# Head norms of the queries as row scales of the softmax, and two reordered activations in the cells of a two-block fp32 layer stack

## The reference

```python
q = rms_norm(q.reshape(b_, t_, ATT_HEADS, ATT_HD), qn_g)      # 8 query heads of 64
k = rms_norm(k.reshape(b_, t_, ATT_KV_HEADS, ATT_HD), kn_g)   # 2 key heads of 64
if tabs is not None:
    q, k = rope_2d(q, tabs), rope_2d(k, tabs)
...
s = jnp.einsum('bqkgd,bskd->bkgqs', q, k).astype(jnp.float32) * (ATT_HD ** -0.5)
p = jax.nn.softmax(s, axis=-1).astype(v.dtype)
```

## Time and profile before

| | |
|---|---|
| median of 3 runs | 3383.92 us (3381.69 to 3394.71) |
| the profiled execution | 3379.07 us, its span 3377.3 us |
| PE busy | 3191.2 us, 94% of the span |
| DVE, ACT, POOL busy | 1307.8, 834.7, 1599.3 us |
| chain that ended last | PE 83%, DVE 9%, POOL 3%, ACT 3%, issue 2% |
| ACT_TABLE_LOAD | 152, of 1283 ns each |

### The profile page before, as it was taken

One profiled execution on the slowest core, in us unless ns is written; L12 is line 12 of the kernel. 1 busy time (PEld: TensorE's weight loads), 2 busy tenths in 40 slices (PEclk: granted clock), 3 DMA queues, 4 the chain that ended last, 5 costly groups with the idle time before them and its releaser, 6 DMA issues.

```text
span 3377.3 us, 40269 instructions
## 1 busy us (share of the span) xinstructions
PE 3191.2 (94%) x15099; PEld 2291.8 (68%) x15099; DVE 1307.8 (39%) x2442; ACT 834.7 (25%) x1479; POOL 1599.3 (47%) x1507
## 2 busy tenths in 40 slices
PE   7999987999999999998989999999999999999988
PEld 4666655656666555465778768888984588889944
DVE  3021325545554412315666543444332334443321
ACT  4123235421111022325411112232110122321110
POOL 1788996000000059961354247775640287765600
PEclk9999989999999999999999999999999999999999
DMA  7111100024444121110234322222221222222211
GB/s 227 40 38 32 38 26 14 14 66 134 125 129 133 40 63 38 44 38 1 72 119 144 96 75 75 63 75 63 76 75 50 64 75 63 76 63 75 74 48 41
DMA packets 259332, 236.59 MB, mean 70 GB/s; under 512 B 20887, under 2 KB 257347, under 8 KB 259141
## 3 DMA queue, kind: packets, MB, share of 16 engines
q1 hardware_dynamic: 259140, 234.02, 22.8%
HBM read 231.91 MB, written 2.10 MB: 69 GB/s over the span
## 4 chain that ended last, share of the span: by engine, by line
PE 83%; DVE 9%; POOL 3%; ACT 3%; issue 2%; DMA 0%; DVEq 0%; ACTq 0%; SPq 0%; POOLq 0%
PE ps L466 29%; PE ps L1140 22%; PE ps L496 10%; PE ps L982 4%; DVE arena L1753 3%; PE ps L1184 2%; ACT arena L1277 2%; PE ps L745 2%; PE ps L1228 1%; PE ps L482 1%; DVE small L1962 1%; DVE bQz L1757 1%; PE ps L1086 1%; POOL arena L2364 1%; PE ps L1220 1%
## 5 line engine op out<-in xcount | busy, mean ns | idle before, releaser
L2364 POOL TENSOR_TENSOR arena<-arena,posi 128x512 f32<-128x512 f32 (+1 forms) x360 | 409.4, 1137 | 30.0
L466 PE MATMUL ps<-hT,wring 128*128 128x512 f32 (+1 forms) x1184 | 411.8, 508 | 1.2 <-ACT arena L1277 1.2
L496 PE MATMUL ps<-hT,wring 128*128 128x512 f32 (+1 forms) x1024 | 373.2, 519 | 1.2 <-ACT arena L1277 1.2
L466 PE MATMUL ps<-arena,wring 128*128 128x512 f32 (+1 forms) x992 | 367.9, 531 | 0.0
L466 PEld LDWEIGHTS ps<-hT,wring 128*128 128x128 f32 x1184 | 230.1, 196 | 169.7 <-issue 153.9
L1277 ACT ACTIVATE arena<-ps 128x256 f32<-128x256 f32 (+4 forms) x403 | 176.4, 438 | 656.2 <-PE ps L466 234.2
L2446 POOL TENSOR_TENSOR arena<-wring 128x512 f32<-128x512 f32 x72 | 92.7, 1288 | 475.5 <-PE ps L1140 292.7
L466 PEld LDWEIGHTS ps<-arena,wring 128*128 128x128 f32 x992 | 187.6, 190 | 175.2 <-issue 168.4
L496 PEld LDWEIGHTS ps<-hT,wring 128*128 128x128 f32 x1024 | 192.5, 192 | 152.3 <-issue 143.5
L1277 ACT ACT_TABLE_LOAD x152 | 195.0, 1283 | 371.8 <-DVE small L2250 85.8
L2363 POOL TENSOR_SCALAR posi<-arena,cols 128x512 f32<-128x512 f32 (+1 forms) x360 | 246.2, 684 | 35.4
(11 more groups left out here) (256 smaller groups left out, 4909.8 us busy)
## 6 DMA issues: line engine op xcount, KB each, us to landing
wring<-in_w_in SPq DMA_DIRECT2D x126, 1024.0 KB, 5.3
wring<-in_w_mod SPq DMA_DIRECT2D x24, 1024.0 KB, 8.3
wring<-in_w_out SPq DMA_DIRECT2D x24, 1024.0 KB, 5.7
wring<-in_w_ada SPq DMA_DIRECT2D x21, 1024.0 KB, 5.2
wring<-in_w_conv_out SPq DMA_DIRECT2D x7, 512.0 KB, 6.1
wring<-in_w_gla_out SPq DMA_DIRECT2D x7, 512.0 KB, 6.2
wring<-in_w_attn_out SPq DMA_DIRECT2D x7, 512.0 KB, 5.5
arena<-in_w_ada SPq DMA_DIRECT2D x3, 1024.0 KB, 5.1
```

Source lines behind the costliest of these rows:

```text
L466: last = eng.matmul(o_(out), a, b_, start=(i == 0), stop=(i == len(parts) - 1))
L496: mm = eng.matmul(bank[b][:, 0:n], w[:, k, j * P:(j + 1) * P], hT[:, k, t0:t0 + n], start=(k == 0), stop=(k == KD - 1))
L2364: pool.link(eng.tensor_tensor(dst, dst, scratch, ALU.add))
```

## The change

Query norms. The queries are no longer multiplied by their inverse root. Their tiles are turned raw, with the gain folded into the permutation (`gperm`), and the gain also goes into the product with the cosine. The inverse roots of all four query tiles (`qscale`, 128 tokens on the partitions by 6 blocks by 8 heads) come from one root and one reciprocal, and are used twice in the attention: the negated row maximum is multiplied by them (`nmax`, a product of 128 x 1 on DVE after each maximum), and ACT's exponential takes them as its scale. The keys stay normed, with one root and one reciprocal for both tiles. The GLA spread moves behind the second query turn, and DVE's products that use it (`gla_scaled`) with it. For the whole stretch the V ring has four banks (`HEAD_RINGS`).

Cells. For mLSTM heads `silu(n, 3)` stands between the two parts of the activation of the gate z instead of behind them. In every chunk ACT takes a root of `eps` into an unused column after it has emptied the chunk's product and before it waits for the variance.

```diff
-        hcol = sb("hcol", [P, 2, 6, 2])
+        kcol = sb("kcol", [P, 2, 6, 2])
+        head_cols = sb("head_cols", [P, NCH * 16])
+        qscale = head_cols[:, 0:48].rearrange("p (a b c) -> p a b c", b=6, c=2)
+        gperm = pt[:, 3, TX:TX + P]
+        k_squares, q_squares = [pt[:, 2, :], last_tile], [pr[:, 0, :], pr[:, 1, :], pt[:, 2, :], last_tile]
...
-        qcol = sb("qcol", [P, NCH, 4, 4])
+        qcol = head_cols.rearrange("p (a b c) -> p a b c", b=4, c=4)
...
-                gla_out_norm(l, 1, between)
+                next(between, None)
+                gla_square_sums(l, 1)
+                rings[0] = HEAD_RINGS
+
+                def head_sums(name, b, tiles_):
+
+                    pe.stage("attn_proj")
+                    key = (name + "ss", l)
+                    claim(b)
+                    eng.wait_ge(*at(("gla out read", l, 1)))
+                    for j in tiles_:
+                        eng.wait_ge(*at(("hsq", l, name, j)))
+                        for u in units(0 if name == "k" else l):
+                            src = (k_squares if name == "k" else q_squares)[j]
+                            last = eng.matmul(bank[b][:, 12 * j + 2 * u:12 * j + 2 * u + 2], src[:, u * P:(u + 1) * P],
+                                              const[:, K_HALF:K_HALF + P:64], start=True, stop=True)
+                    last.then_inc(*pe.tell(("full", key)))
+                    bank_of[key], last_on[b] = bank[b], key
+
...
+                            for i, u in enumerate(UNITS[sg]):
+                                for hf in range(2):
+                                    last = eng.matmul(o_[64 * hf:64 * hf + 64, i * P:(i + 1) * P],
+                                                      kcol[:, j, u, hf:hf + 1].broadcast_to([P, 64]), ident,
+                                                      start=True, stop=True)
+                            return last
+                        eng.wait_ge(*at(("k inverse", l)))
+                        job("V", ("hbc", l, j, sg), mms)
...
+                    pe.stage("attn_proj")
+                    if name == "k":
+                        src, perm = ak[:, j, TC:T], const[:, K_PERM:K_PERM + P]
+                        eng.wait_ge(*at(("normed", l, j)))
+                    else:
+                        src, perm = res[:, 8 + j, TC:T], gperm
+                        eng.wait_ge(*at(("q perm", l)))
+                        eng.wait_ge(*at(("free", ("aq", l, j, segs(l)[-1]))))
+                    job("V", ("rot", l, name, j), lambda o_: eng.matmul(o_[:, 0:TX], perm, src, start=True, stop=True))
+
+                head_sums("k", 4, (0, 1))
+                next(between, None)
+                key_norms(0)
+                key_norms(1)
+                turned("q", 0)
+                next(between, None)
+                turned("k", 0)
+                turned("k", 1)
+                head_sums("q", 7, range(4))
+                turned("q", 1)
+                next(between, None)
+                gla_spread(l, 1)
+                turned("q", 2)
+                next(between, None)
+                turned("q", 3)
                 pe.stage("attn_proj")
-
-                for t in range(len(HEAD_TILES) + 2):
-                    if t < len(HEAD_TILES):
-                        name, j = HEAD_TILES[t]
-
-                        def mms(o_):
-                            for u in units(0 if name == "k" else l):
-                                last = eng.matmul(o_[:, 2 * u:2 * u + 2], sq[t % 2][:, u * P:(u + 1) * P],
-                                                  const[:, K_HALF:K_HALF + P:64], start=True, stop=True)
-                            return last
-                        eng.wait_ge(*at(("hsq", l, name, j)))
-                        job("A", ("hss", l, name, j), mms)
-                    if t % 2:
-                        next(between, None)
-                        pe.stage("attn_proj")
...
@@ -1393,10 +1428,16 @@
                         fn(gsq[hh][:, t0:t0 + n].rearrange("p (a b) -> p a b", b=GLA_CHUNK), src, ACT.Square)
                     m.mark(("gla sq", l, 2 * p + hh), act.name, act.n[act.name])
                 m.mark(("gla out read", l, p), act.name, act.n[act.name])
+                if p:
+                    for j in range(2):
+                        fn(k_squares[j], ak[:, j, :], ACT.Square, ("hsq", l, "k", j))
                 next(between, None)
                 act.stage("gla_norm")
                 for hh in range(2):
                     evac(("gss", l, 2 * p + hh), gcol[:, hh, u0:6], u0, 6 - u0, ACT.Sqrt, scale=1.0 / P, bias=eps[:, :])
+                if p:
+                    act.stage("attn_proj")
+                    evac(("kss", l), kcol.rearrange("p a b c -> p (a b) c"), 0, 24, ACT.Sqrt, bias=eps[:, :])
...
+                eng.wait_ge(*at(("q inverse", l)))
+
                 def probabilities(n, e):
                     i = first + n
+                    sg, hp, qb = pairs[n]
+                    r = qscale[:, hp, UNITS[sg][qb], e:e + 1]
...
-                    fn(dst, src, ACT.Exp, ("probs", i, e), bias=small[:, 40 + z:41 + z], accum_out=small[:, 44 + z:45 + z])
+                    fn(dst, src, ACT.Exp, ("probs", i, e), scale=r, bias=small[:, 40 + z:41 + z], accum_out=small[:, 44 + z:45 + z])
...
-                for t in range(len(HEAD_TILES) + 2):
...
-                        if t > 1:
-                            eng.wait_ge(*at(("full", ("hss", l, *HEAD_TILES[t - 2]))))
-                        fn(sq[t % 2][:, u0 * P:T], src[:, u0 * P:T], ACT.Square, ("hsq", l, name, j))
-                        if t > 1:
-                            for sg in both if HEAD_TILES[t - 2][0] == "k" else segs(l):
-                                eng.wait_ge(*at(("full", ("hbc", l, *HEAD_TILES[t - 2], sg))))
-                        evac(("hss", l, name, j), hcol[:, t % 2, u0:6, :], 2 * u0, 12 - 2 * u0, ACT.Sqrt, bias=eps[:, :])
-                    next(between, None)
+                u0 = units(l)[0]
+                act.stage("attn_proj")
+                for j in range(4):
+                    src, dst = res[:, 8 + j, u0 * P:T], q_squares[j][:, u0 * P:T]
+                    fn(dst, src, ACT.Square, ("hsq", l, "q", j))
+                next(between, None)
+                act.stage("attn_proj")
+                eng.wait_ge(*at(("full", ("qss", l))))
+                src = bank_of["qss", l][:, 0:48].rearrange("p (a b) -> p a b", b=12)[:, :, 2 * u0:12]
+                fn(qscale.rearrange("p a b c -> p a (b c)")[:, :, 2 * u0:12], src, ACT.Sqrt, ("free", ("qss", l)), bias=eps[:, :])
...
                             evac(key, zt_flat[:, 0:HALF], 0, HALF, ACT.Silu)
+                            if not r:
+                                silu(n, 3)
                             eng.wait_ge(*at(("free", ("right", (l, n, i)))))
                             fn(zt_flat[:, HALF:], zt_flat[:, HALF:], ACT.Silu, ("gate z", l, n))
-                        if not r and i:
+                        if not r and 0 < i < 4:
                             silu(n, i - 1)
...
                         evac(("intra", k), NI[:, 0:W], 0, W)
+                        fn(small[:, 90:91], eps[:, :], ACT.Sqrt)
                         eng.wait_ge(*at(("var", k)))
                         fn(small[:, 56:57], small[:, 55:56], ACT.Sqrt, ("sd", k), bias=eps[:, :])
...
-                            dve.link(eng.tensor_reduce(small[:, 40 + z:41 + z], src, ax, ALU.max, negate=True), ("nmax", i, e))
+                            nmax = small[:, 40 + z:41 + z]
+                            sg, hp, qb = pairs[n]
+                            dve.link(eng.tensor_reduce(nmax, src, ax, ALU.max, negate=True))
+                            tt(nmax, nmax, qscale[:, hp, UNITS[sg][qb], e:e + 1], M_, ("nmax", i, e))
...
-                    out_norm(l, p)
-                m.mark(("branch", l, 1), *m.at[("gla out done", l, 1)])
+                    if p == 0:
+                        out_norm(l, p)
...
+                gain = small[:, 20 + l:21 + l]
+                ts(gain, col(l, QN), 0.125, None, M_, None)
+                eng.wait_ge(*at(("gla core", (l, 1, 1))))
+                ts(gperm, const[:, K_PERM:K_PERM + P], gain, None, M_, None, ("q perm", l))
+                gla_inverse(l, 1)
+                dve.stage("rope")
+                eng.wait_ge(*at(("free", ("kss", l))))
+                rcp(kcol[:, :, :, :], kcol[:, :, :, :], ("k inverse", l))
+                for j in range(2):
+                    for sg in ("x", "c"):
+                        s0, n = SEG[sg]
+                        k = ("hbc", l, j, sg)
+                        eng.wait_ge(*at(("full", k)))
+                        stt(ak[:, j, s0:s0 + n], bank_of[k][:, 0:n], col(l, KN), ak[:, j, s0:s0 + n], M_, M_, ("free", k))
...
+                def rotated(name, j):
+                    dve.stage("rope")
+                    src = ak[:, j, :] if name == "k" else res[:, 8 + j, :]
+                    k = ("rot", l, name, j)
```

(26 more changed lines are left out.)

## The result

| | before | after | predicted |
|---|---|---|---|
| median of runs | 3387.8 us (4 runs) | 3355.47 us (4 runs, 3351.97 to 3356.32) | 3341 |
| after : before | | 0.99, 95% interval 0.9887 to 0.9914 | 0.9873 |
| profiled execution, its span | 3379.07, 3377.3 | 3351.97, 3350.0 | -42.3 |

The kernel is faster by 1.0% (0.9 to 1.1%). The ratio 0.9873 is 3341 over the 3383.92 from which it was worked out. From span to span the kernel gained 27.3 us, where the sum of the prediction had 42.3. One profiled execution of an experiment, that of tapfirst, ran slower than its other three (3425.5 us, at a mean granted clock of 0.93), so the median of tapfirst is of three runs and it has no stages.

A forecast was written before the change was run, and what follows sets the result against it. PE, busy 94% of the span, was taken as the bound. 33 + 9.6 - 18 + 10 + 7.7 = 42.3 us off 3379.07 gave 3336.8; with 4.85 for the median, 3341 us, range 3318 to 3367.

The forecast's parts named there:

- Layer 0, head stretch: Layer 0 ahead of the attention: new order without PE waits saves 36.5 us, less 2 x 1.8 for the clock: 33.
- Layer 1, head stretch: Layer 1 ahead of the attention: DVE ends last, first transposes 13.2 us earlier, less 3.6 for the clock: 9.6.
- Attention, layer 1: Layer 1's attention: two new products per step in the loop of DVE and scores, 15 steps, cost 6 us.
- Attention, layer 0: Layer 0's attention: products, some beside POOL's taps, cost 12 us; both layers together 18, bounds 8 and 30.
- Cells, the activation: Cells: moving `silu(n, 3)` into ACT's idle time removes 10 of 12.4 us of PE's waits at the scores.
- rival 2: Cells give nothing, because what waits next (POOL's weight sums, DVE's chunk) ends at the same time: 3359; 15%.
- Cells, the root: End of a chunk in the cells: the added root saves the table load's 1.28 us in six waits, 7.7 us.
- Rival 1: Clock stays low in both layers' gate tiles, turns and spreads; gain falls by about 29 us: 3370; 10%.
- Rival 3: Products are cheap and the clock holds: attention costs 8 instead of 18, 7 us of clock not lost: 3324; 17%.
- rival 4: Slower than before: all 80 attention products at their worst row, 1.22 us plus 0.03, cost 100 us: 3424; 3%.

The follow-up runs named there:

- tapfirst: The changed kernel with POOL's last tap of a head ahead of the weight sums for the next head's first tile; 3344.3 us.
- early: The changed kernel with the GLA norm's spread and last three query turns ahead of gate tiles on PE, GLA scaling earlier on DVE, both layers; 3356.3 us.
- twice: The changed kernel with every product of the attention made twice, the second into a column nobody reads; 3373.2 us.
- bare: The changed kernel without the 80 products on DVE and with constant 1 as the exponential's scale; 3336.5 us.
- actprod: The changed kernel with the product moved from DVE to ACT, as a Copy ahead of each exponential; 3340.7 us.
- warm: The changed kernel with ten more small matmuls on PE in each triple of layer 0's attention, ahead of the waits for scores; 3357.7 us.
- root_only: The kernel before with only the added root of a constant ahead of the wait for the variance in the cells; 3378.6 us.
- best0: The changed kernel with the product as a Copy on ACT, POOL's last tap ahead of the next weight sums, and early's order in layer 1 alone; 3317.0 us.

## Why the prediction was right, and where it was not

The forecast's mechanism came, inside its range, but 14 us above its value. By its steps:

- **Layer 0, head stretch: right**, -30.8 for -33. The waits cost nothing, as taken, but for one of 0.83 at the first scores. The clock took some 7 us (3.0 and 1.4 in the two gate tiles, 1.8 in the sums: 3.18 and 6.40 for 7.8, and 1.0 in the turn behind them) where I took 3.6 from the earlier trace rows: the clock was low in more pieces than the two tiles that I counted.
- **Layer 1, head stretch: right**, -8.9 for -9.6: DVE ended last, as said; early, which moves DVE's work, moved the end. The closeness of the number is in part luck, as this stage scatters by 3 to 4 us from kernel to kernel.
- **Attention, layer 1: right**, +5.3 for +6. The product took 160 ns, the cheapest row; twice added 5.1 more.
- **Attention, layer 0: mis-sized**, +17.0 for +12. Beside the taps a product took 443 ns and 0.03, a little more than my 0.4, but the taps lay beside 24 products and not 30, and the others took 160. All 48 are 16.2 us with what stood idle before them, by my own factor of 2/3 10.8. What I left out is that a longer wait lowers the clock: PE was busy 6.5 us more for the same matmuls, and the one fall that can be priced by itself cost 1.5. bare and actprod, where the waits and the falls are gone together, and warm, where two falls go with more matmuls, bear it out. The bound of 30 held both.
- **Cells, the activation: the step that failed.** "POOL's last tap is done before the second part of z can start" is true of the kernel before, and of the activation alone (9 us less waiting, for my 10). But the root lets PE and ACT arrive 1.87 us earlier and POOL not, and the margin was 1.47: POOL's tap became the last, and 6.7 us of waiting stayed. I had given such a case 15% as rival 2, for both edits at once; it came for 6.7 of their 17.7 us.
- **Cells, the root: right in place**, a little more than its wait: 9.9 us of waits gone for 7.7. The 1.28 of the load is gone, and DVE's scaling behind it took 0.77 in place of 1.40. It ends about 0.15 us behind the POOL instruction beside it in each kernel (2121.85 and 2122.01 before, 2126.71 and 2126.86 in root_only), so this part hangs on where POOL is. With the two, 1.28 and 0.63, the rows cover each wait of 1.64. The Trainium skill (ScalarE: Activation LUTs, "What ACT_TABLE_LOAD costs") puts a switch at 2.66 us, by which all six waits would go too; the 9.9 alone doesn't tell it from the rows' account.

Rival 1 (the clock stays low) had a point: the clock of layer 0's stretch rose only from 0.89 to 0.91. It cost some 7 us there and not 29 in both, as only the pieces behind small matmuls were slow. Rival 3 was wrong about the clock, rival 4 about the price: 301 ns on the mean of layer 0, not 1.22 us. (The sum gives 3336.8 + 4.85 = 3341.6, so 3342; nothing hangs on it.)

Open: why the clock falls after one wait of 1.49 in the cells and not after the next (in best0 it falls once in each block behind no wait at the scores), and which part of the run of small matmuls makes a gate tile slow. No run tells them apart.

## What to carry to other kernels

Two edits that each take away a wait on the same path need not add up: work out the second with the arrival times that the first leaves, and look at every engine that doesn't get faster. An instruction of 0.2 us inside a loop of two engines costs its whole time at each turn (layer 1's step grew by 0.39 for two of them); put it on the engine whose result is used a step later (here ACT, 15 us). And a wait that grows on PE costs more than itself, if the clock falls behind it.

## What the runs showed of the hardware

A product of 128 x 1 on DVE with both inputs in SBUF took 160 ns alone and 443 on the mean (159 to 1115) beside POOL's taps; as a tensor_scalar with a pointer, 214 either way. As a Copy on ACT it took 295 on the mean. PE's clock fell behind waits of 3.4, 2.5 and 1.84 us in the attention (but not behind each of 1.84), and a fall cost 1.5; ten small matmuls put in ahead of the wait took the last two of these three away, and the stage was 3.6 us shorter for it.
